# Two lanes for the recurrence: the inverses of both directions level by level, with the gate tiles placed anew

## The reference, cut to what matters

```python
def step(state, inp):
    r_t, w_t, k_t, v_t, a_t, b_t = inp
    sa = jnp.einsum('bhvk,bhk->bhv', state, a_t)
    state = (state * w_t[:, :, None, :] + sa[..., None] * b_t[:, :, None, :]
             + v_t[..., None] * k_t[:, :, None, :])
    return state, jnp.einsum('bhvk,bhk->bhv', state, r_t)
...
y_f = wkv7_scan(r_h, decay_h[:, :, 0], k_dir[:, :, 0], v_h, -kk, kk * a_h[:, :, 0])
y_b = fl(wkv7_scan(fl(r_h), fl(decay_h[:, :, 1]), fl(k_dir[:, :, 1]), fl(v_h),
                       fl(-kk), fl(kk * a_h[:, :, 1])))
y = y_f + y_b
...
gates = jax.nn.sigmoid(z_gate + gate_b[l])
mixed = gates[:, :, 0] * (o_mla @ w_br_mla[l]) + gates[:, :, 1] * (o_rwkv @ w_br_rwkv[l])
x = x + mixed @ w_out[l]
```

## Time and profile before

| what | value |
|---|---|
| median of 3 runs | 2014.22 us (2009.97 to 2017.88) |
| span of the profiled execution | 2017.2 us |
| TensorE busy | 1920.1 us, 95% |
| VectorE, ScalarE, GpSimd busy | 885.4, 414.9, 826.9 us |
| stretch of the recurrence, first lora to the start of the merge's main part | 1449.7 to 1696.1 us |
| TensorE busy in it | 222.7 of 246.4 us |
| clock granted to TensorE over the span, and in this stretch | 0.98 and 0.88 of 2.4 GHz |

### The profile page before, as it was taken

One profiled execution on the slowest core, in us unless ns is written; L12 is line 12 of the kernel. 1 busy time (PEld: TensorE's weight loads), 2 busy tenths in 40 slices (PEclk: granted clock), 3 DMA queues, 4 the chain that ended last, 5 costly groups with the idle time before them and its releaser, 6 DMA issues.

```text
span 2017.2 us, 45982 instructions
## 1 busy us (share of the span) xinstructions
PE 1920.1 (95%) x19510; PEld 1663.8 (82%) x19510; DVE 885.4 (44%) x2014; ACT 414.9 (21%) x1043; POOL 826.9 (41%) x858
## 2 busy tenths in 40 slices
PE   7999999999999999999999999999999898889898
PEld 4999988889999999998878999997877777644454
DVE  4576544545552377533463433125554444311112
ACT  2111032342110111113243211012433210110011
POOL 2888731007888787953100788900122200001110
PEclk9999999999999999999999999999997899999999
DMA  9799833415775499843332345533311011999995
GB/s 391 271 319 350 303 115 106 149 62 198 252 251 179 168 333 335 312 136 126 117 126 76 136 169 180 172 128 115 104 65 44 24 47 63 374 412 402 351 381 205
DMA packets 111360, 405.81 MB, mean 201 GB/s; under 512 B 13888, under 2 KB 14144, under 8 KB 110400
## 3 DMA queue, kind: packets, MB, share of 16 engines
q1 hardware_dynamic: 87408, 325.61, 44.6%
q10 hardware_dynamic: 19152, 71.05, 10.1%
q0 software_dynamic: 4608, 6.31, 0.9%
HBM read 445.91 MB, written 1.05 MB: 222 GB/s over the span
## 4 chain that ended last, share of the span: by engine, by line
PE 82%; DMA 6%; DVE 5%; issue 3%; POOL 2%; ACT 1%; SPq 0%; DVEq 0%; POOLq 0%; ACTq 0%
PE ps L867 27%; PE ps L912 12%; PE ps L1368 7%; PE ps L2073 4%; PE ps L3408 3%; PE ps L2155 3%; PE ps L2554 2%; PE ps L3434 2%; PE ps L3392 2%; DMA ring<-in_experts_down 2%; DMA arena<-in_weights 1%; PE ps L3445 1%; DMA ring<-in_weights 1%; PE ps L1365 1%; PE ps L2206 1%
## 5 line engine op out<-in xcount | busy, mean ns | idle before, releaser
L867 PE MATMUL ps<-sq,arena 128*128 128x128 f32 x2112 | 250.3, 275 | 0.0
L831 POOL TENSOR_TENSOR arena<-ring 128x512 f32<-128x512 f32 (+1 forms) x176 | 175.6, 998 | 170.5 <-PE ps L867 105.2
L867 PEld LDWEIGHTS ps<-sq,arena 128*128 128x128 f32 x2112 | 242.9, 192 | 0.1
L867 PE MATMUL ps<-h,ring 128*128 128x128 f32 x1408 | 178.3, 279 | 6.3 <-DVE h L791 3.5
L836 POOL TENSOR_TENSOR arena<-ring,arena 128x512 f32<-128x512 f32 (+1 forms) x176 | 176.8, 1005 | 13.8
L834 POOL TENSOR_TENSOR arena<-arena,ring 128x512 f32<-128x512 f32 (+1 forms) x176 | 179.1, 1018 | 0.0
L832 POOL TENSOR_TENSOR arena<-ring 128x512 f32<-128x512 f32 (+1 forms) x176 | 176.1, 1001 | 0.0
L867 PEld LDWEIGHTS ps<-h,ring 128*128 128x128 f32 x1408 | 167.7, 193 | 9.7 <-ACT h L653 4.5
L912 PE MATMUL ps<-arena 128*128 128x128 f32 x1408 | 173.6, 275 | 0.0
L1368 PE MATMUL ps<-h,ring 128*128 128x256 f32 x768 | 172.2, 381 | 0.0
L912 PEld LDWEIGHTS ps<-arena 128*128 128x128 f32 x1408 | 165.3, 192 | 0.0
(11 more groups left out here) (585 smaller groups left out, 3175.1 us busy)
## 6 DMA issues: line engine op xcount, KB each, us to landing
ring<-in_weights SPq DMA_DIRECT2D x427, 512.0 KB, 4.1
arena<-in_weights ACTq DMA_DIRECT2D x86, 512.0 KB, 5.3
arena<-in_experts_up SPq DMA_DIRECT2D x16, 2048.0 KB, 15.6
ring<-in_experts_up SPq DMA_DIRECT2D x16, 2048.0 KB
cst<-in_weights ACTq DMA_DIRECT2D x42, 512.0 KB, 5.3
arena<-in_experts_down SPq DMA_DIRECT2D x8, 2048.0 KB, 13.9
ring<-in_experts_down SPq DMA_DIRECT2D x8, 2048.0 KB
cst<-in_consts ACTq DMA_DIRECT2D x1, 1860.0 KB, 10.0
```

The source lines that it names most:

```text
L831: pool.tensor_tensor(to[:, 0], a21, a22, ALU.add).then_inc(S("sum_one"), 1)
L867: mm = pe.matmul(into, weight[:, k], moving[:, k], start=(k == 0), stop=(k == half - 1))
```

## The change

The recurrence goes in two lanes. Lane 0 has the calls of direction 0, lane 1 those of direction 1; each lane has its own buffers, semaphores (`inv_sem`) and PSUM banks for the inverse. The order of TensorE is now:

- `lora` 0 and 1, V turned, four half gate tiles, bonus 0, a half tile, `tok(0)`, then `all_pairs(0)`, a half tile, `tok(1)`, `all_pairs(1)`, with a half tile inside each. `all_pairs` lets the w and y products of two heads (`first_values`) follow their masks, in place of one group behind all four
- the inverses of calls 0 and 1 level by level: P1 of both, a half tile, XP of both, a half tile
- u, y and state of calls 0 and 1, with two half tiles; then all pairs of calls 2 and 3 with a half tile between
- the inverses of calls 2 and 3 likewise, with nine half tiles and four branch tiles
- u and y of calls 2 and 3, then the end as before

`held` now accumulates in PSUM into the same bank as w, and the VectorE addition is gone. `m12` is two small buffers, zeroed once, in place of one that GpSimd zeroed before each call. VectorE's two memsets at the start go to GpSimd. `sig` and `dd` of call 1 have buffers of their own, so `scan(1)` need not wait for call 0. ScalarE takes the exponentials of calls 0 and 1 together, behind the gates of the first four half tiles.

```diff
-    FILL = (("p", "0", 2), ("p", "0b", 4), ("p", "1", 2), ("p", "2", 1), ("p", "3", 1), ("p", "4", 1), ("p", "5", 1),
-            (0, "1a", 1), (0, "2a", 1), (0, "2b", 1), (0, "3a", 1), (0, "3b", 1), (0, "4a", 1), (0, "5a", 1), (0, "6a", 1),
-            (1, "2b", 1), (1, "3b", 1), (1, "5a", 1), (1, "6a", 1),
-            (2, "1c", 1), (2, "2b", 1), (2, "3b", 1), (2, "5a", 1), (2, "6a", 1), (2, "7", 1), (3, "1c", 1), (3, "2b", 1))
-    TILES = ((3, "2c"), (3, "3b"), (3, "3c"), (3, "4c"), ("t", "u"), ("t", "y"), ("t", "centre"), ("t", "var"))
+    FILL = (("p", "start", 4), ("p", "tok", 1), ("p", "pair", 1), ("p", "between", 1), ("p", "last", 1),
+            (0, "1a", 1), (0, "1c", 1), (0, "2a", 1), (0, "2c", 1), (0, "3a", 1), (0, "3c", 1), (0, "4a", 1), (0, "4c", 1), (0, "5a", 1), (0, "5c", 1),
+            (0, "6a", 1), (0, "6c", 1),
+            ("m", "u", 1), ("m", "y", 1), ("m", "last", 1),
+            (1, "1a", 1), (1, "1c", 1), (1, "2a", 1), (1, "2c", 1), (1, "3a", 1), (1, "3c", 1), (1, "4a", 1), (1, "4c", 1), (1, "5a", 1))
+    TILES = ((1, "4a"), (1, "5a"), (1, "5c"), (1, "6a"), ("t", "u"), ("t", "y"), ("t", "centre"), ("t", "var"))
...
+        def all_pairs(n, between=()):
+            pairs(n, 0)
+            for name in between:
+                fill("p", name)
+            pairs(n, 1)
+            if n >= 2:
+                held(n)
+            first_values(n, 0)
+            for ct in (2, 3):
+                pairs(n, ct)
+                first_values(n, ct - 1)
+            first_values(n, 3)
...
+        for s in range(2):
+            calls = (call_of(2 * s), call_of(2 * s + 1))
             for level in range(1, INV_LEVELS):
...
+                for call, d, _, _ in calls:
...
+                    inv_p1_pe(pe, call, d, level)
+                fill(s, f"{level}a")
+                branch_tile(s, f"{level}a")
+                for call, d, _, _ in calls:
+                    inv_xp_pe(pe, call, d, level, 0)
+                    inv_xp_pe(pe, call, d, level, 1)
+                    if (s, level, d) == (0, 1, 1):
+                        lora(2)
+                    if (s, level, d) == (0, 3, 1):
+                        lora(3)
+                    if (s, level, d) == (0, 5, 1):
+                        bonus(2)
+                fill(s, f"{level}c")
+                branch_tile(s, f"{level}c")
+            if s == 0:
+                fresh(0)
+                fresh(1)
+                fill("m", "u")
+                output(0)
+                output(1)
+                fill("m", "y")
+                state(0)
+                state(1)
+                bonus(3)
+                all_pairs(2)
+                fill("m", "last")
+                all_pairs(3)
...
         sigmoids(1, 0)
         sigmoids(1, 1)
-        gates("p", "1")
+        gates("p", "start")
+        exponents(0)
+        exponents(1)
+        gates("p", "bonus")
+        gates("p", "tok")
         tok(0)
```

More of the change, by code:

```diff
@@ L1146, in inv_masks_pool @@
         v = inv_bufs(call)
-        base = 2 * (INV_LEVELS - 1) * call
+        turn = inv_turn(call)
+        _, base = inv_base(call)
         for b in range(2):
@@ L1180, in inv_p1_pe @@
                     for q in quarter:
[L1181 removed]
+                        mm = pe.matmul(inv_p1_bank(call, b)[q, SUB * m:SUB * m + SUB], v["lb"][level % 2][q, b, m], v["xx"][q, b, 0, m], start=True, stop=True)
                 elif level == INV_SMALL:
@@ L2726, in rwkv_pe @@
+        for call, _, _, _ in calls:
+            pe.wait_ge(inv_sem("x_updated", call), 2 * INV_LEVELS * (inv_turn(call) + 1))
         for ct in range(4):
@@ L2834, in rwkv_act @@
         diagonal(0, 1)
[L2835 removed]
         first_w(0)
         y_from_v(0)
[L2838 to L2859 removed]
+        gates("p", "between")
@@ new lines, in rwkv_act @@
+        tok(1)
+        gates("p", "last")
+        diagonal(1, 0)
+        diagonal(1, 1)
+        first_w(1)
+        y_from_v(1)
+        for s in range(2):
+            calls = (call_of(2 * s), call_of(2 * s + 1))
+            for level in range(1, INV_LEVELS):
+                for call, d, _, _ in calls:
+                    inv_level_act(act, call, d, level)
+                if s == 0:
+                    if level <= 2:
+                        sigmoids(2, level - 1)
+                    elif level == 3:
+                        exponents(2)
+                    elif level <= 5:
+                        sigmoids(3, level - 4)
+                for slot in "ac":
+                    gates(s, f"{level}{slot}")
+            if s == 0:
+                exponents(3)
+                fresh(0)
+                fresh(1)
+                gates("m", "u")
+                gates("m", "y")
+                diagonal(2, 0)
+                diagonal(2, 1)
+                first_w(2)
+                gates("m", "last")
+                diagonal(3, 0)
+                diagonal(3, 1)
+                first_w(3)
@@ L2860, in rwkv_act @@
+        fresh(2)
         fresh(3)
@@ new lines, in rwkv_dve @@
+        bonus(0)
+        for ct in range(4):
+            pairs(0, ct)
+        raw(1)
+        operands(1)
+        for ct in range(4):
+            pairs(1, ct)
+        bonus(1)
+        for s in range(2):
+            calls = (call_of(2 * s), call_of(2 * s + 1))
+            for level in range(INV_LEVELS):
+                for call, d, _, _ in calls:
+                    inv_level_dve(dve, call, d, level)
+                if s == 0:
+                    if level == 2:
+                        scan(2)
+                    elif level == 3:
+                        centred(2)
+                        direction(2)
+                    elif level == 4:
+                        raw(2)
+                    elif level == 5:
+                        operands(2)
+                        scan(3)
+                        centred(3)
+                        bonus(2)
+                for slot in "ac":
+                    branch_out(s, f"{level}{slot}")
+            if s == 0:
+                direction(3)
+                raw(3)
+                operands(3)
+                add_y(0, output_bank(0), "y")
+                add_y(1, output_bank(1), "y")
+                state(0)
+                state(1)
+                bonus(3)
+                for ct in range(4):
+                    pairs(2, ct)
+                add_y(2, 3, "yv")
+                for ct in range(4):
+                    pairs(3, ct)
+                add_y(3, 3, "yv")
```

519 lines of the change are left out of this document (217 added, 302 removed), and 4 rows, old and new, of the table wkv_steps.

## The result

The changed kernel took 2035.13 us in the median (2026.96 to 2036.23, 4 runs) against 2012.73 (2009.97 to 2017.88, 4 runs) for the kernel before: ratio 1.0096, 95% interval 1.0073 to 1.012. It is slower by about 1%, where I had forecast 2002 us and faster. (Medians differ by some us from series to series, so each ratio compares with the runs of the kernel before in the same series.)

What follows compares the result with a forecast made beforehand. TensorE's matmul work, gaps and clock bound the kernel; 198 work + 12 clock loss + 24.6 idle = 234.6 against 246.4 us, 11.8 less, gives 2002 us from the 2014.2 median. Range 1988 to 2016.

Steps and rivals of the forecast that it cites:

- With issue gaps 5: TensorE gaps named issue between first lora and merge stay at 5 us, part of 24.6 us idle.
- The clock: Slow time at prologue, openings, middle and tail: 27 us at the lower clock, 12 us lost.
- prologue: Before the first pairs: TensorE waits 1.7 us for exponentials and products, 1.4 us for tok's copies; together 3.1 us.
- openings: Start of each inverse pair: four level-0 updates in a row on VectorE make TensorE wait 2.8 and 3.5 us, 6.3 together.
- tail: End of the recurrence: VectorE's level 5, branch product and last update make TensorE wait 2.0 us.
- I let waits below 1 us cost nothing: Clock step: TensorE waits shorter than 1 us bring no fall of the clock, so 0 us for them.
- last head pairs: Masked copies on VectorE outlast TensorE's work at the last head pair: 0.8 to 0.9 us, four times, 3.5 us.
- levels: Inverse levels: each lane's matmuls and half tiles cover the other lane's copies and updates; only 1.1 us of waits.
- The lanes do not remove idle time; they gather it: From first lora to merge, TensorE's idle time is 24.6 us against 23.7 before.
- C: Rival, chance 0.10: clock falls inside packed levels over XP and the half tile; 2.7 us a level, 2034 us for all.
- B: Rival, chance 0.21: waits and slow time only moved; idle 28, slow time near 50 us; 2016 us, half of it 2008 to 2010.
- the milder half of B: Short waits at the last four head pairs each bring 3.5 us of slow time: 6 us more, 2008 us.

Runs made afterwards that it cites:

- e7_turn_spread: Changed kernel with XP's second product of levels 1 to 4 replaced by a VectorE transpose and each half gate tile of the levels cut in two: 1994.8 us.
- e11_lanes: The two-lane kernel with the VectorE transpose for XP's second product and half tiles in two pieces, measured again: 1994.98 us.
- e9_mix: Changed kernel plus 24 rounds of 120 small (32x32) and 8 large (128x256) matmul records before a P1 group in the second pass: 2123.3 us.
- e12_single: The kernel before, calls one after the other, with XP's second product replaced by a VectorE transpose, measured again: 2004.44 us.
- e10_mix2: Changed kernel plus 24 rounds of 112 small (32x32) and 16 large (128x256) matmul records before a P1 group in the second pass: 2147.1 us.
- e6_long: Changed kernel plus one unbroken run of 1536 small matmul calls (3072 records) behind a P1 group in the second pass: 2121.5 us.

## Why the prediction was wrong

**The step that failed** is "With issue gaps 5": I took the gaps named "issue" over from the old order as a constant, without asking what ends them. They measured 24.8 us, and the runs above show them to be waits for the next block of instructions. It was to be had from the rows: I had written that a pass of both lanes is 8 us of work and that XP is 2.7 us of 32x32 matmuls. The instruction queue was on the page before too, with the same 154 packets, and the 1.51 us gap named "issue" inside XP ends at 1606.13, 1.2 us before a packet at 1607.4: the pattern of the long run. By the floor a level is 3.1 x 3.6 = 11.3 us in place of 8, in eight levels 26 us of gaps. That is close to what came, though the sum takes a level as a whole and the floor holds for each block by itself, so the closeness is in part luck. The old order had the same number of records, but its levels shared their time with lora, pairs, w, u and states, so that a block seldom ended early.

**The clock** was the second miss, and it hangs on the first. I had 27 us slow and 12 lost; it was 57 slow, and 219 - 198 = 21 lost, if the work stayed 198. Of the nine issue gaps of 1.6 us and more, seven stand less than 2 us ahead of a fall of the clock or across it, and one in slow time that had begun before; the ninth, 2.98 us before 1632.47, has full clock behind it, and so have the four up to 1.0 us. Those seven slow pieces, which begin in levels 1 to 4, are some 34 us together. The other slow time of the stretch, some 25 us, begins at the prologue wait, at the two openings, at the tail and at the merge, about where I had placed my 27. The counter-test is e7_turn_spread and e11_lanes: with most of the gaps gone the slow time is 22 us. So the size of the clock forecast holds for the order that I had priced, one without these gaps.

One step of it doesn't hold: "I let waits below 1 us cost nothing". Windows around two falls of the kernel after, then around one of the kernel before:

```profile
1496.00:1497.70 1.70, 1.70 (x16) 1.46 (x16) 0.00 (x0) 1.51 (x5) 0.89 (x3) 1.00 0.00 0
1497.80:1499.10 1.30, 0.04 (x1) 0.00 (x0) 1.19 (x4) 0.18 (x1) 1.30 (x4) 0.50 0.00 0
1672.00:1675.20 3.20, 2.48 (x34) 2.08 (x32) 3.02 (x13) 1.13 (x3) 0.00 (x0) 1.00 0.13 54
1675.40:1678.60 3.20, 3.02 (x7) 2.49 (x8) 0.46 (x2) 0.34 (x1) 0.00 (x0) 0.50 0.03 5
```
```profile
1637.00:1642.00 5.00, 4.29 (x95) 3.63 (x86) 1.02 (x3) 0.55 (x2) 0.82 (x2) 1.00 0.01 3
1642.30:1645.50 3.20, 3.20 (x71) 2.71 (x71) 0.42 (x1) 0.60 (x1) 0.00 (x0) 0.50 0.00 0
```

The clock is down at 1497.8, where the wait of the first opening only begins; the only wait in the 12 us ahead is the 0.58 us at the last head pair, before 1495.82. In the 10 us ahead of 1675.3 there are 0.72 us of waiting, in the 5 us ahead of 1642.2 in the kernel before 0.71 us. Against that stand 2.98 us before 1632.47, 1.51 us before 1606.13 and 0.73 us four times in e9_mix, all with full clock behind them. The length of a gap alone doesn't decide; what does, these runs leave open.

**Waits**, forecast against measured:

| | forecast | after |
|---|---|---|
| prologue (L3017, L2860, opening) | 3.1 | 3.4 + 1.3 + 0.4 |
| last head pairs (L3049) | 3.5 | 4 x 0.58 = 2.3 |
| openings (L1268) | 6.3 | 3.6 + 1.1 = 4.7 |
| levels | 1.1 | 0 |
| middle | 0 | 0 |
| tail | 2.0 | 0.7 + 0.6 + 0.2 = 1.6 |

14 us against 16.0: the prologue took 2 us more than forecast, the openings (2.1 and 2.6 us) and the last head pairs less. Two lanes do cover each other, as the step "Levels" said: no P1 or XP of levels 1 to 4 waits for another engine, the openings apart. "The lanes do not remove idle time; they gather it" holds for e11_lanes, 21.4 us idle against 22.7 in e12_single. The last stretch before the merge kept its 3.6 us.

**The sum again**: 198 + 12 + 24.6 = 234.6 was forecast; 198 + 21 + 41.9 = 260.9 is what the trace has. Of the 26 us, 20 are issue gaps, 9 clock, and the other waits give 2.5 back.

**The rivals.** C named the right time, 2034 us, and the right place, XP of both lanes and the half tile behind it, and its sign came, slow pieces inside levels 1 to 4. But its mechanism, that small matmuls by themselves lower the clock, is not what runs show: level 2 of the first pass after has the same 256 records of XP, a gap of only 0.36 us, and half tiles of 1.99 us behind; and in e10_mix2 112 small records a round ran at full clock from 1616.5 on. That C hit the time is luck. B was right that the slow time stays near 50 us and idle goes over 28, for a reason that it didn't have. None of them asked whether TensorE gets its instructions in time, and the chance of 0.10 for slower was too small because all cases shared that blind spot. The Trainium skill, "TensorE: Matmul & The Clock Gate", section "A second HAM failure mode: psum-queue depth-cycling", has micro-idles between groups, which I kept as the milder half of B; that would have brought slow pieces behind the four 0.58 us waits at the last head pairs. Behind the first and the third there is none, behind the second there is one (the windows above), and the fourth stands just ahead of an opening, from which it can't be told. So the trace doesn't speak against that half as plainly as I had written.

## What to carry to other kernels

Count instructions, not only columns: a matmul with its load is two, a float32 call here two of each, and in these runs 256 instructions took at least 3.5 us on TensorE, each such block by itself. Before packing small matmuls together, add up how many records stand in each run; keep 128 records from being worth less than that time, by parting them with large matmuls or by giving some to an idle engine (e7_turn_spread did both). A gap named "issue" in the middle of a group of equal matmuls is the sign.

## What the hardware showed unexpectedly

- TensorE's instructions came in blocks of 256 with 3.5 to 4.0 us from one to the next (mean 3.66 in e6_long) at 2% DMA load, and no more than one block lay ready.
- Two scans on VectorE beside products of GpSimd took 1.42 us each, one on the same buffers without GpSimd 0.39, four beside GpSimd's memsets 0.40 to 0.43 each.
- The clock fell behind seven of nine issue gaps of 1.6 us or more and behind none of four shorter ones; yet two falls of the same stretch had no more than 0.58 and 0.72 us of waiting ahead, and in e9_mix gaps of 0.2 to 0.7 us every 3.5 to 4 us left the large matmuls at 1.99 us.
